# A hybrid decoder step on one core: key scores as summed multiplies, the prompt's attention interleaved head by head, SiLU and squares of query and key inside the last head, first value pages between norm sums and broadcasts

## The reference, cut to what is computed

```python
fq, fk, fv, ff, gconv, gz, ga, gb = split(u @ w_in)        # 28 chunks of 128 columns and the gates
# fox attention of the prompt: 4 heads of 128, causal, with a forget gate
s = q @ k.T * scale + c[:, None] - c[None, :]               # c = cumsum(logf)
o = softmax(s masked) @ v
# fox attention of the samples: 8 samples x 16 cached pages x 128 rows, picked by page_table
rc = cumsum(lp, reverse) - lp                               # gates of the cached rows behind this one
s_past = (q . k_page) * scale + cn + rc
o = softmax([s_past, s_new]) @ [v_page, v]
# gated delta rule: 12 channels of 128 (4 query, 4 key, 4 value)
c = silu(causal_conv(gconv, 4 taps));  q, k = l2norm(q) * 128**-0.5, l2norm(k)
# chunks of 64: (A + I) X = rhs with A strictly lower triangular, then state and output
```

## Time and profile before

| | us |
|---|---|
| median of 3 runs | 2692.89 (2690.4 to 2698.13) |
| the profiled execution's own time | 2685.75 |
| its span in the trace | 2683.5 |
| PE busy in the span | 2533.7 (94%) |
| POOL busy | 1679.7 (63%) |
| DVE busy | 1373.5 (51%) |
| ACT busy | 542.4 (20%) |

### The profile page before, as it was taken

One profiled execution on the slowest core, in us unless ns is written; L12 is line 12 of the kernel. 1 busy time (PEld: TensorE's weight loads), 2 busy tenths in 40 slices (PEclk: granted clock), 3 DMA queues, 4 the chain that ended last, 5 costly groups with the idle time before them and its releaser, 6 DMA issues.

```text
span 2683.5 us, 53449 instructions
## 1 busy us (share of the span) xinstructions
PE 2533.7 (94%) x20127; PEld 2425.6 (90%) x20127; DVE 1373.5 (51%) x1381; ACT 542.4 (20%) x806; POOL 1679.7 (63%) x711
## 2 busy tenths in 40 slices
PE   7999998996588989999999999999999989999997
PEld 7999997994366779999999999999998889999997
DVE  4444336997853365444344444356676653444433
ACT  3222101003332212222012221012322221222101
...
GB/s 123 89 92 97 98 74 116 249 225 97 105 130 189 193 94 87 94 89 103 86 107 94 86 94 96 97 74 122 97 113 114 97 104 87 93 89 91 101 86 64
DMA packets 472370, 290.97 MB, mean 108 GB/s; under 512 B 32785, under 2 KB 438411, under 8 KB 472270
## 3 DMA queue, kind: packets, MB, share of 16 engines
...
## 4 chain that ended last, share of the span: by engine, by line
PE 76%; DVE 9%; issue 5%; POOL 3%; DMA 2%; ACT 2%; ACTq 1%; DVEq 1%; SPq 0%; POOLq 0%
PE ACC L758 66%; PE ACC L973 3%; POOL WLO L696 2%; DMA RAW<-in_ab_w_in 1%; POOL WHI L693 1%; PE ACC L990 1%; DVE TB L2156 1%; DVE PROD L1711 1%; DMA SSR<-in_state_ret_S 1%; DVE SSR L2073 1%; PE ACC L966 1%; PE ACC L1202 0%; DVE XL L1613 0%; PE ACC L1212 0%; PE ACC L1236 0%
## 5 line engine op out<-in xcount | busy, mean ns | idle before, releaser
L693 POOL TENSOR_TENSOR WHI<-RAW,ZERO 128x1024 fp32r<-128x1024 f32 (+1 forms) x341 | 693.8, 2035 | 636.9 <-PE ACC L758 593.3
L696 POOL TENSOR_TENSOR WLO<-RAW,WHI 128x1024 fp32r<-128x1024 f32 (+1 forms) x341 | 956.1, 2804 | 48.1
L758 PE MATMUL ACC<-XH,WHI 128*128 128x260 f32 x4032 | 823.5, 285 | 10.0 <-POOL WLO L696 5.8
L758 PE MATMUL ACC<-XH,WLO 128*128 128x260 f32 x4032 | 813.8, 284 | 0.0
L758 PE MATMUL ACC<-XL,WHI 128*128 128x260 f32 x4032 | 812.5, 283 | 0.0
L758 PEld LDWEIGHTS ACC<-XH,WHI 128*128 128x128 f32 x4032 | 624.7, 189 | 30.2 <-issue 17.6
L758 PEld LDWEIGHTS ACC<-XH,WLO 128*128 128x128 f32 x4032 | 622.9, 189 | 0.0
L758 PEld LDWEIGHTS ACC<-XL,WHI 128*128 128x128 f32 x4032 | 621.7, 189 | 0.0
L758 PE MATMUL ACC<-HH,WHI 128*128 128x260 f32 x1408 | 284.5, 283 | 1.1 <-POOL WLO L696 1.1
L758 PE MATMUL ACC<-HH,WLO 128*128 128x260 f32 x1408 | 283.4, 283 | 0.0
L758 PE MATMUL ACC<-HL,WHI 128*128 128x260 f32 x1408 | 282.8, 282 | 0.0
...
## 6 DMA issues: line engine op xcount, KB each, us to landing
...
```

What stands on the lines that cost most here:

```text
L693: pool.tensor_tensor(WHI[:, slot, 0:nk, :], RAW[:, slot, 0:nk, :], ZERO[:, :].broadcast_to([P, nk, P]), ALU.add).then_inc(hi_split, 1)
L696: pool.tensor_tensor(WLO[:, slot, 0:nk, :], RAW[:, slot, 0:nk, :], WHI[:, slot, 0:nk, :].bitcast(F32), ALU.subtract).then_inc(split, 1)
L758: ins = pe.matmul(ACC[acc][:, n, 0:HALF], w[:, slot, k, :], a[:, k0 + k, n * HALF:(n + 1) * HALF], start=first and opens, stop=final and c ...
```

## The change

The first mixer is reordered; the rest of the kernel is the same.

- A key batch becomes 16 instructions of 128 columns (`scalar_tensor_tensor`) that multiply a page's head with the query's broadcast in PSUM and sum the row into one column of SC by `accum_out`. All 32 batches stand beside the 24 projection units; KPAGES has three slots, and ACT issues all loads. QBR, PROD and the selector are gone: the PE broadcasts the query from the identity into bank 4 or 6.
- `later`, `total` and the suffix sums move into the projections' loop, one step for each unit (`later_pages`). The loops of 8 are written out.
- Heads overlap: QS, KT, VT, PROB and STAT exist twice, the scores of head h+1 stand between turn and values of head h, and the samples' softmax is interleaved with head 0. The chunks are read from PRJ without copies KS and VS.
- The convolution leaves the DVE: ACT makes three shifted, scaled copies and scales the channel in place (`conv_taps`), POOL adds (`convolve`; the samples' columns in `convolve_samples`). SiLU of query and key runs in four parts inside the last head.
- SP loads the first four value turns ahead of the heads, and the PE multiplies them between the norm's sums and its broadcasts, which now use two accumulators.
- In the levels of the delta rule the product XT becomes four transposes of the new XI (`level_turn`), which ACT copies to XIT. The last level works on 64x64 corners alone (`corner_t`, `corner_xt`). The samples' state is read one level later, behind ACT's copies. The values turn that stood behind the state's product is moved behind the corners.

```diff
...
         KBATCH = 4
-        EARLY = 6
+        KEY_UNITS = AB_CH - 4
+        KEY_BATCHES = DEC * N_PAGES // KBATCH
+        def batches(n):
+            return range(KEY_BATCHES * n // KEY_UNITS, KEY_BATCHES * (n + 1) // KEY_UNITS)
...
-        KPAGES = [at(f"KPAGES{n}", [P, 2, KBATCH, FOX_HEADS * P], a) for n, a in enumerate((mo_at, ring_at))]
-        PROD = [at(f"PROD{n}", [P, KBATCH, FOX_HEADS * P], a + PAGES_BYTES) for n, a in enumerate((mo_at, ring_at))]
+        K_SLOTS = 3
+        KPAGES = at("KPAGES", [P, K_SLOTS, KBATCH, FOX_HEADS * P], mo_at)
+        Q_BANK = (4, 6)
...
-        def load_keys(engine, store, slot, first, n):
-            hold(engine, prod_done, n + 1)
+        def load_keys(engine, slot, first, n):
+            if n >= K_SLOTS:
+                engine.wait_ge(prod_done, n + 3 - K_SLOTS)
             for g in range(KBATCH):
                 page = engine.value_load(PT_SB[0:1, bass.ds(first + g, 1)], min_val=0, max_val=N_POOL - 1)
-                engine.dma_start(KPAGES[store][:, slot, g, :], cache_k[0, bass.ds(page, 1)].rearrange("a t h d -> (a t) (h d)"))\
+                engine.dma_start(KPAGES[:, slot, g, :], cache_k[0, bass.ds(page, 1)].rearrange("a t h d -> (a t) (h d)"))\
...
-            with sp.Fori(0, FOX_HEADS) as h:
-                for m in range(2):
-                    load_keys(sp, 1, m, N_PAGES * (EARLY + m) + KBATCH * h, 4 * EARLY + 2 * h + m)
...
             for turn in range(V_SLOTS):
                 load_values(sp, turn, turn, turn)
-            sp.wait_ge(fs_dve.sem, FOX_PROBS)
+            for h in range(FOX_HEADS):
...
+            def convolve(c):
+                pool.wait_ge(cv_tap, c + 1)
+                for shift in range(1, CONV_W):
+                    if shift > 1:
+                        await_step(pool, cv_pool, f"add{shift - 1}", c)
+                    out = PRJ[:, AB_CONV + c, shift:SEQ]
+                    cv_pool.done(pool.tensor_tensor(out, out, CONV_TILES[c % 2][shift - 1][:, shift:SEQ], ALU.add), f"add{shift}")
...
+            convolve_samples()
+            for c in range(CONV_CH):
+                convolve(c)
             pool.wait_ge(lev_in, 16)
             for p in range(PAIRS):
-                for n in range(1, LEVELS):
+                for n in range(1, LEVELS - 1):
...
-                hold(pe, selb_ready, b + 1)
-                pe.matmul(bank(4), SELB, QTOK, start=True, stop=True).then_inc(qb_ready, 1)
...
+                pe.matmul(bank(Q_BANK[b % 2]), IDENT[0:DEC, b:b + 1].broadcast_to([DEC, P]), QTOK, start=True, stop=True).then_inc(qb_ready, 1)
...
-            with pe.Fori(0, (AB_CH - 4) // 8) as i:
-                for m in range(8):
-                    project_ab(8 * i + (m + 4), m)
-                    if m in (0, 4):
-                        broadcast_q(2 * i + (m // 4 + 1))
-            broadcast_q(EARLY + 1)
+            for n in range(AB_CH - 4):
+                project_ab(n + 4, n + 4)
+                for i in batches(n + 2) if n + 2 < KEY_UNITS else ():
+                    if i > 0 and i % KBATCH == 0:
+                        broadcast_q(i // KBATCH)
+                if n == 2:
...
+                    fs_pe.done(pe.matmul(bank(7), LATER[:, :], lf, start=True, stop=True), "later")
+                    fs_pe.done(pe.matmul(bank(5), ONES[:, :], lf, start=True, stop=True), "total")
...
+            for h in range(FOX_HEADS):
+                if 0 < h < FOX_HEADS - 1:
+                    fox_tokens(h + 1)
                 for q in range(NBLK):
-                    score(q)
-                for q in range(NBLK):
-                    turn(q)
-                    values(q)
...
+                    fox_turn(h, q)
+                    if h + 1 < FOX_HEADS:
+                        score(h + 1, q)
+                    if h == 0 and q == 0:
+                        pe.wait_ge(fs_dve.sem, fs_dve.value("dn"))
+                        fs_pe.done(pe.matmul(bank(6)[:, 3 * P:3 * P + NDH], ONES[:, :], DEN[:, :, :].rearrange("p b h -> p (b h)"), start=True, stop=True), "den")
+                        pe.wait_ge(fs_dve.sem, fs_dve.value("den"))
+                    fox_values(h, q)
...
+            ln_pe.done(ins, "sum")
+            for _ in range(V_SLOTS):
+                values()
+            pe.wait_ge(ln_dve.sem, ln_dve.value("inv"))
+            for j in range(2 * GDN_HEADS):
...
-                    await_step(pe, gl_dve, f"xt{n - 1}{q}", p)
-                    if n < LEVELS - 1:
-                        gl_pe.done(per_head(bank_of(q, 1), lambda h: XIT[q][:, h, :], lambda h: T1[q][:, h, :]), f"x{n}{q}")
-                    gl_pe.done(per_head(bank_of(q, 2), lambda h: T1[q][:, h, :], lambda h: XIT[q][:, h, :]), f"xt{n}{q}")
+                    if n > 1:
+                        await_step(pe, gl_act, f"xt{n - 1}{q}", p)
+                    else:
+                        await_step(pe, gl_dve, f"xt0{q}", p)
+                    gl_pe.done(per_head(bank_of(q, 1), lambda h: XIT[q][:, h, :], lambda h: T1[q][:, h, :]), f"x{n}{q}")
+                def level_turn(n, q):
+                    await_step(pe, gl_dve, f"x{n}{q}", p)
+                    for h in range(GDN_HEADS):
+                        ins = pe.transpose(bank(bank_of(q, 2))[:, h * P:(h + 1) * P], XI[q][:, h, :], IDENT[:, :])
+                    gl_pe.done(ins, f"xt{n}{q}")
+                def corner_t(q):
+                    for h in range(GDN_HEADS):
+                        ins = pe.matmul(bank(bank_of(q, 0))[HB:P, h * HB:(h + 1) * HB], AT[q][0:HB, h, HB:P], XI[q][0:HB, h, 0:HB],
+                                        start=True, stop=True)
+                    gl_pe.done(ins, f"t{LEVELS - 1}{q}")
+                def corner_xt(q):
+                    await_step(pe, gl_act, f"t{LEVELS - 1}{q}", p)
+                    await_step(pe, gl_act, f"xt{LEVELS - 2}{q}", p)
+                    for h in range(GDN_HEADS):
+                        ins = pe.matmul(bank(bank_of(q, 2))[0:HB, h * HB:(h + 1) * HB], T1[q][HB:P, h, 0:HB], XIT[q][HB:P, h, HB:P],
+                                        start=True, stop=True)
+                    gl_pe.done(ins, f"xt{LEVELS - 1}{q}")
...
+                    for q in range(2):
+                        level_turn(n, q)
+                        if n + 1 < LEVELS - 1:
+                            level_t(n + 1, q)
+                        else:
+                            corner_t(q)
...
-                    values()
...
-            def select(b):
-                act.activation(SELB, IDENT[0:DEC, bass.ds(b, 1)].broadcast_to([DEC, P]), ACT.Copy).then_inc(selb_ready, 1)
-            def keep_q(b, parity, multiplied):
-                hold(act, qb_ready, b + 1)
-                hold(act, prod_done, multiplied)
-                act.activation(QBR[:, parity, :], bank(4), ACT.Copy).then_inc(qbr_ready, 1)
...
+            for n in range(KEY_BATCHES):
+                load_keys(act, n % K_SLOTS, KBATCH * n, n)
...
-            act.activation(channels(GQ, 2 * GDN_HEADS), channels(GQ, 2 * GDN_HEADS), ACT.Silu).then_inc(cv_act, 1)
...
+            def conv_taps(c):
+                source = PRJ[:, AB_CONV + c, :]
...
+                for shift in range(1, CONV_W):
+                    tap = PAR_CONV + CONV_CH * (CONV_W - 1 - shift) + c
+                    ins = act.activation(CONV_TILES[c % 2][shift - 1][:, shift:SEQ], source[:, 0:SEQ - shift], ACT.Copy, scale=PAR[:, tap:tap + 1])
+                ins.then_inc(cv_shifted, 1)
+                act.wait_ge(cv_shifted, c + 1)
+                tap = PAR_CONV + CONV_CH * (CONV_W - 1) + c
+                act.activation(source[:, 0:SEQ], source[:, 0:SEQ], ACT.Copy, scale=PAR[:, tap:tap + 1]).then_inc(cv_tap, 1)
...
+            for h in range(FOX_HEADS):
+                if 0 < h < FOX_HEADS - 1:
+                    fox_query(h + 1)
+                    fox_keys(h + 1)
+                for q in range(NBLK):
+                    fox_turned(h, q)
+                    if h + 1 < FOX_HEADS:
+                        exponent(h + 1, q)
+                    if q < NBLK - 1:
+                        conv_taps(3 * h + q)
+                    if h == FOX_HEADS - 1:
+                        part = channels(GQ + 2 * q, 2)
...
+                        act.wait_ge(cv_pool.sem, cv_pool.value("add3", 2 * q + 1))
+                        act.activation(part, part, ACT.Silu).then_inc(cv_act, 1)
+                await_step(act, fb_pe, "pv3", h)
+                fb_act.done(act.activation(MOH[:, h, 0:SEQ], bank(VALUE_BANK), ACT.Copy), "hi")
...
+            act.wait_ge(cv_act, 4)
             ln_act.done(act.activation(SQH[:, 0:GDN_HEADS, :], channels(GQ, GDN_HEADS), ACT.Square), "sqq")
             ln_act.done(act.activation(SQH[:, GDN_HEADS:, :], channels(GK, GDN_HEADS), ACT.Square), "sqk")
+            act.wait_ge(cv_pool.sem, cv_pool.value("add3", CONV_CH - 1))
             act.activation(channels(GV, 2 * GDN_HEADS), channels(GV, 2 * GDN_HEADS), ACT.Silu).then_inc(cv_act, 1)
...
```

(43 more changed lines are left out.)

514 lines of the change are left out of this document (263 added, 251 removed).

## The result

The changed kernel took 2621.28 us (median of 4 runs, 2615.91 to 2623.89) against 2692.7 for the kernel before; the ratio is 0.9729, 95% interval 0.9707 to 0.9751. The time fell by 71 us where 39 were forecast. It lies inside the range of 2612 to 2716, but only because that range takes in rival B's 2616; the forecast's own range, 2630 to 2683, missed it. The profiled execution took 2619.68 us with a span of 2617.9, so 66 us less than the profiled one of before.

What follows compares the result with a forecast made beforehand. In the projections PE, DVE, POOL and DMA were taken to be near their limits together. Terms +38.3 - 55.8 - 21.5 = -39.0 us gave 2646.8 us (2654 against the median); range 2612 to 2716, own range 2630 to 2683.

Steps and rivals of the forecast that it cites:

- rival B: Key scores: the sum is free, keys end at 609 us, +0 in place of +38, total 2616 us; chance 0.17.
- The keys: Key scores beside the projections: last key at 647.5 us against 609.2 before, +38.3 us.
- key pair: A key score's multiply and the read of its sum on the DVE: 0.334 us each, 171 us for 512.
- The DMA floor: Projections: loading 12.6 MB of weights and 33.6 MB of keys takes 152 us, so keys cannot end before about 607.
- Rival C: Key scores: read and next multiply wait for each other; 2714 us at 0.45 us a pair, 2758 at 0.536; chance 0.19.
- POOL freed: Projections: POOL, freed of the multiply, has its subtraction well under 4.26 us and hides under the DVE.
- From the last key to the delta rule: Stretch between key scores and delta rule: 22 + 54 + 27 = 103 us against 158.8, so -55.8 us.
- The way to the heads: From the last key to the head loop: the sample's softmax chain with head 0's first steps in its waits, 22 us.
- The heads: Four attention heads bound by ACT: 14 us each, 12 for head 0, with 1.6 us of waits; sum 54 us.
- Rival D: Heads stay near 20 us through engine handshakes and POOL's additions colliding with the DVE's normalizing: 2678 us; chance 0.10.
- The norms: Sums, value turns and broadcasts ahead of the delta rule: 27 us in all, 11 of them for the broadcasts.
- The delta rule: Two chunk pairs: -5.7 us each from the levels, 12.6 us of ACT waits removed, 2.5 given back; together -21.5 us.

Runs made afterwards that it cites:

- E1: Changed kernel with the key scores' factor 1.0 taken from a column of a tile instead of a constant: 2631.97 us (0.9781).
- E2: Changed kernel with the key scores' second output, the sums by row, left out and the multiplies kept: 2626.98 us (0.9766).
- E3: Changed kernel with a key batch as one 2048-column multiply, query still in PSUM, and one 2048-column reduction: 2635.91 us (0.9796).
- E6: Changed kernel with ACT's convolution copies ahead of the next head's exponential instead of behind it: 2612.52 us (0.9701).
- E5: Changed kernel with POOL's three additions of a channel on the first columns alone (shift to 8 instead of 512): 2624.35 us (0.9742).
- E11: Changed kernel with the edits of E6, E9 and E10, and head 1's first two row maxima moved ahead on the DVE: 2601.97 us (0.9676).
- E7: Changed kernel with SiLU of query and key in one piece behind the last head instead of four parts inside it: 2624.99 us (0.9754).
- E4: Changed kernel with the first four value turns behind the norm's broadcasts instead of ahead of them: 2632.36 us (0.9787).
- E10: Changed kernel with ACT's first two odd page loads ahead of its wait for the norm's last multiply: 2619.12 us (0.973).
- E9: Changed kernel with ACT's copy of the first pair's second value sum ahead of the last level's copies and page loads: 2612.29 us (0.9702).

## Why the prediction was right or wrong

**The keys: wrong in size, 41.6 us.** The step was the price of a key pair, 0.2585 + 0.075 = 0.334 us. Both parts were too high. The 0.2585 came from an instruction with a column as its scalar, and the column is 0.061 of it (E1, E2). The 0.075 was the spacing of two 128x1 instructions, about the length of a read, but a read starts together with the next multiply; 0.010 is left (E2). With 0.208 the DVE needs 107 us for 512 key pairs, the PE's projections set the pace, and the keys end at 605.1, even below the 609 of rival B. B's sum was all but free, as B had it, but B's 609 rested on the same 0.2585: that the time came out near B's 2616 is in part luck, for the other stages gave less than forecast. The DMA floor of 607 was no floor either: the projections' window moved 41 MB (292 GB/s in 141.7 us) of the 46 that it counted, and the rest had been loaded before. The Trainium skill (VectorE: DVE Perf Modes, section on two Vector instructions with no wait between them) has the sum's read as a second instruction; the trace agrees, with a record of 0.08 us. The other rule of the Trainium skill (VectorE: DVE Perf Modes, The DRAIN you can't avoid), that the next operation starts when the pipe is empty, comes with an exception for operations that are not held, which the forecast left out; these rows agree with the exception, since the next multiply and the read both start 0.08 us before the multiply ends (455.50 and 455.58). Rival C fell with that.

**POOL freed: right**, 2405 ns in the changed kernel as in E3, and its reason was one operand in PSUM.

**From the last key to the delta rule: near in sum (110.0 for 103), wrong in its parts.** The way to the heads took 13.8 us for 22: the keys end late on the DVE, but the PE makes head 0's scores meanwhile. The chain that ended last, in order of time, goes there past the keys, over the PE's scores (L945, L946):

```profile
...
597.73 0.71 DVE PRJ L1823
...
604.30 0.86 PE ACC L945 x2
605.16 0.86 PE ACC L946 x2
...
606.24 0.89 PE ACC L972 x8
...
```

The heads took 70.7 us for 54. ACT's work was right (12.9 for 12.4), its waits were not: 4.3 us in a head for 1.6, because an exponential stood ahead of copies that could have been made in its wait (E6). Rival D had the size better (17 to 19 us a head), but not the reason: without POOL's additions a head takes the same time (E5). Only in E6's first head did that collision decide something. The first head took 19.3 for 12, at a clock of 0.65; until 627.9, almost half of it, ACT and the PE waited for row maxima behind small steps of the samples' softmax, and with those maxima moved it took 14.8 (E11). The last one took 16.9 for 14; what SiLU costs inside it is what it saves behind it but for 0.5 to 1.8 us (E7).

**The norms: right in sum** (25.5 for 27). I took 11 us for the broadcasts, because nothing showed that the wait set the clock; E4 shows that filling it makes the difference (E5 is the exception), and 7.8 is the price at the upper level, not the 7.1 of the halved time. The sums ahead of them took 9.9 us for 8.8, at a clock of 0.71.

**The delta rule: right in the levels, too hopeful in the first pair.** A level takes 6.7 us in the second pair for 6.9, and that pair gained 7.1 us for 5.7. The first gained 9.2 for 15.8: the give-back by the two early page loads was allowed at 2.5 us and cost 4.6 (E10), and the bank of the second value sum was overlooked, 5.6 (E9). "No PE wait on ACT in the first pair" was wrong at these two places.

So the sign was right, and so was that the middle gains more than the pairs (48.5 and 16.3 us). The keys' term was not: it was to cost 38.3 us and gave 3.3. The time lies 33 us below the forecast and 5 above rival B's. In the profiled spans (2617.9 against 2683.5 less 39.0) it is 26.6 below: 41.6 are the keys, and the other way go 7.0 of the middle, 5.2 of the pairs and 3.4 behind them (what is left is the first take, 0.8 us earlier, and rounding).
